# A hybrid decoder layer on one core, with and without six groups of constant products on TensorE

## The reference

```python
u = rmsnorm(x)
h = x + concat(gated_delta_net(u), rg_lru(u)) @ w_out       # 4 heads of 128; 4 blocks of 128
h = h + cross_attention(rmsnorm(h), rmsnorm(mem))           # 4 heads, 256 memory tokens
h = h + moe(rmsnorm(h))                                     # top 4 of 32 clamped-SwiGLU experts
out = rmsnorm(h)

def expert_block(x, e):                                     # blocks of 128 rows of one expert
    gt = minimum(x @ w_gate[e] + b_gate[e], 7.0)
    up = clip(x @ w_up[e] + b_up[e], -7.0, 7.0)
    return ((up + 1.0) * (gt * sigmoid(1.702 * gt))) @ w_down[e] + b_down[e]
```

## Time and profile before

| | us |
|---|---|
| median of 3 executions | 1771.23 |
| lowest, highest | 1770.09, 1771.25 |
| profiled execution, its own time | 1772.93 |
| span of the profiled execution | 1771.2 |
| TensorE busy | 1690.2 (95%) |
| VectorE busy | 1437.0 (81%) |
| ScalarE busy | 1274.6 (72%) |
| GpSimd busy | 527.8 (30%) |

### The profile page before, as it was taken

How to read it: one execution, slowest core, us unless ns; L and a number is a source line. 1 busy time by engine, 2 the same in 40 slices (tenths; PEclk the granted TensorE clock), 3 DMA queues, 4 the chain that set the end, 5 groups by cost and what they waited for, 6 DMA issues and landing times.

```text
span 1771.2 us, 24520 instructions
## 1 busy us (share of the span) xinstructions
PE 1690.2 (95%) x8065; PEld 1385.7 (78%) x8065; DVE 1437.0 (81%) x1531; ACT 1274.6 (72%) x1452; POOL 527.8 (30%) x624
## 2 busy tenths in 40 slices
PE   6999799899899989999999999999999999999997
PEld 3778598787768768888888888888888888888885
DVE  3558686663347969999999999999999999999997
ACT  4453454464435668888888888888888888888885
POOL 3453552200022822242222222232232323232232
PEclk9999999999998989999999999999999999999999
DMA  7312100042014879999999999999999999999993
GB/s 249 119 51 100 41 1 1 24 190 95 26 82 191 330 271 369 360 383 378 355 371 371 382 359 370 360 382 379 351 371 369 379 364 369 360 380 379 353 371 120
DMA packets 53880, 476.18 MB, mean 269 GB/s; under 512 B 10503, under 2 KB 11640, under 8 KB 29266
## 3 DMA queue, kind: packets, MB, share of 16 engines
q1 hardware_dynamic: 42528, 450.70, 62.8%
q0 software_dynamic: 11120, 24.91, 6.3%
q10 hardware_dynamic: 194, 0.06, 0.0%
HBM read 461.24 MB, written 23.08 MB: 273 GB/s over the span
## 4 chain that ended last, share of the span: by engine, by line
PE 61%; DVE 18%; issue 12%; ACT 6%; POOL 3%; DMA 1%; ACTq 0%; POOLq 0%; DVEq 0%
PE ps L1546 20%; PE ps L1506 17%; PE ps L1143 10%; PE ps L1304 4%; DVE wsp L1888 4%; DVE extra L2058 2%; DVE extra L2056 2%; DVE wsp_b L1888 2%; ACT extra L1048 2%; POOL extra L608 1%; PE ps L1533 1%; PE ps L1227 1%; DVE wf L1616 1%; PE ps L1239 1%; PE ps L1496 1%
## 5 line engine op out<-in xcount | busy, mean ns | idle before, releaser
L1888 DVE TENSOR_TENSOR wsp<-ring,wsp 128x1024 fp32r<-128x1024 f32 x512 | 601.1, 1219 | 26.6 <-ACT wsp L1003 26.1
L1003 ACT ACTIVATE wsp<-ring 128x1024 fp32r<-128x1024 f32 x388 | 387.0, 1051 | 80.2 <-PE ps L1488 53.0
L580 POOL TENSOR_TENSOR guard<-guard 1x1 f32<-1x1 f32 x219 | 133.8, 616 | 763.0 <-ACT extra L1071 327.9
L1506 PE MATMUL ps<-wsp,x_hi 128*128 128x512 f32 x1152 | 311.8, 392 | 0.6 <-DVE x_lo L2014 0.6
L1888 DVE TENSOR_TENSOR wsp_b<-ring,wsp_b 128x1024 fp32r<-128x1024 f32 x256 | 301.8, 1218 | 9.8 <-ACT wsp_b L1081 9.1
L1506 PEld LDWEIGHTS ps<-wsp,x_hi 128*128 128x128 f32 x1152 | 217.5, 189 | 50.1 <-issue 1.1
L1003 ACT ACTIVATE wsp_b<-ring 128x1024 fp32r<-128x1024 f32 x194 | 205.5, 1060 | 32.3 <-PE ps L1506 11.0
L1506 PE MATMUL ps<-wsp,x_lo 128*128 128x512 f32 x576 | 179.1, 392 | 0.0
L1616 DVE TENSOR_TENSOR wf<-ring,wf 128x1024 fp32r<-128x1024 f32 x64 | 81.3, 1273 | 111.8 <-ACT wf L713 111.8
L713 ACT ACTIVATE wf<-ring 128x1024 fp32r<-128x1024 f32 x80 | 84.2, 1055 | 117.4 <-PE ps L1143 62.2
L1143 PE MATMUL ps<-act_hi,wf 128*128 128x512 f32 x512 | 161.6, 397 | 2.6 <-DVE wf L1616 2.1
(11 more groups left out here) (380 smaller groups left out, 2993.9 us busy)
## 6 DMA issues: line engine op xcount, KB each, us to landing
ring<-in_w_gate_dram SPq DMA_DIRECT2D x32, 4096.0 KB, 15.3
ring<-in_w_up_dram SPq DMA_DIRECT2D x32, 4096.0 KB, 14.4
ring<-in_w_down_dram SPq DMA_DIRECT2D x32, 4096.0 KB
ring<-in_w_in_dram SPq DMA_DIRECT2D x6, 2048.0 KB, 12.0
ring<-in_w_ckv_dram SPq DMA_DIRECT2D x4, 2048.0 KB, 10.1
ring<-in_w_out_dram SPq DMA_DIRECT2D x2, 2048.0 KB, 10.6
ring<-in_w_cq_dram SPq DMA_DIRECT2D x2, 2048.0 KB, 11.1
ring<-in_w_co_dram SPq DMA_DIRECT2D x2, 2048.0 KB, 10.6
```

What stands on the lines that cost most here:

```text
L580: return pool.tensor_tensor(guard[:, i:i + 1], guard[:, 0:1], guard[:, 0:1], ALU.mult)
L1003: act.activation(split_w(c, 0), ring[:, m, k], ACT.Copy).then_inc(hi_ready, 1)
L1506: last = pe.matmul(ps[:, 2 * j + i], xp[:, k * P:(k + 1) * P], split_w(c, part)[:, i * 512:(i + 1) * 512], start=False, stop=(k == KT - 1 ...
L1888: dve.tensor_tensor(split_w(c, 1), ring[:, (GM + c // KT) % 3, c % KT], split_w(c, 0), ALU.subtract).then_inc(lo_ready, 1)
```

## The change

The helper and its six calls are taken out. The waits before and behind them stay, in their order, and so does every other instruction.

```diff
-            def fill_wait(n, bank):
-
-                for _ in range(n):
-                    pe.matmul(ps[:, bank, 0:2 * P], sel[:, 0], sel[:, :, :].rearrange("p j f -> p (j f)"), start=True, stop=True)
-
@@ heads of the delta net, h == 1
                     pe.wait_ge(kd_in, 1)
-                    fill_wait(30, 0)
@@ ahead of the solve's first transposes
             pe.wait_ge(kd_in, H)
-            fill_wait(34, 0)
@@ ahead of mixer_out(2)
             pe.wait_ge(orms_ready, H)
-            fill_wait(24, 0)
@@ i == 4
                     pe.wait_ge(onorm_ready, H)
-                    fill_wait(14, 4)
                     pe.wait_ge(al_ready, A_DN)
@@ cross attention
-            fill_wait(20, 6)
             prob_transposes(NT - 1)
@@ behind the router
-            fill_wait(12, 1)
             pe.wait_ge(oh_ready, 1)
```

## The result

Without the products the kernel takes 1773.28 us (median of 14; 1772.60 to 1775.39), with them 1770.19 us (median of 14; 1767.47 to 1772.71). The ratio is 1.0019, 95% interval 1.0011 to 1.0027: slower by 3.1 us between the medians, 1.9 to 4.8 us by the interval. In the profiled executions the spans are 1771.6 and 1771.2 us, only 0.4 apart. The profiled execution of the kernel before took 1772.93 us, 2.7 above the median of its fourteen and above the slowest of them; that of the changed kernel took 1773.40, 0.1 above its median. So this pair of profiles shows where time is lost, and not how much the change costs.

What follows compares the result with a forecast made beforehand. Bound: a full TensorE for two thirds, started by a serial front part of some 630 us. Terms 1.9 + 1.2 + 0.9, dropping the 0.1 us direct gain, made 4.0 us: 1771.23 to 1775.2 us, range 1771.0 to 1781.0.

Steps and rivals of the forecast that it cites:

- No direct gain: All six waits: the 18.4 us of products hide under other engines' work; removing them gives back at most 0.1 us.
- Group 1: 30 products ahead of the second head's key products: without them the clock falls and heads run at half rate, 1.9 us.
- this work is one third transposes, so I allow it one and a half heads: Heads from 198.1 us: how many run at half clock, averaging 0.8 us for one and 3.1 for two into 1.9.
- Group 5: 20 products at 477.37 us: eight transposes behind them 0.9 us slower, products of L1395 0.3 us more; together 1.2 us.
- Executions in which the fall doesn't happen today: Behind groups 4 and 5: where the clock holds today, the change costs 1.7 us more; at one in four each, 0.9.
- Groups 2, 3, 4: 34 products done at 212.1 us, 24 at 308.36, 14 at 317.52: slower work there stays covered by waits; cost 0.
- four stretches: TensorE at half clock (1.2 GHz) at 217.3 to 224.0, 323.1 to 326.4, 483.6 to 486.8 and 627.6 to 633.6 us.
- Group 6: 12 products at 561.72 us: L1458 starts cold, but L1474 ends just in time for VectorE's L2018; cost 0, upper bound 4.4.
- Whatever the front part loses arrives at the end one for one: Serial front part of some 630 us: its delays pass on whole, as the loop has 4 us in 1000 to give back.
- B: Rival, heads behind 198.1 us and L1395: low clock outlasts mixed work, 1778.7 us, or 1783.1 with a later bound; chance 0.22.
- C: Rival, 311.9 to 322.92 us: earlier fall shortens the idle, so 48 products run warm; faster, 1769.4 us; chance 0.06.
- A: Rival, not measurably slower: one cold head 0.8 us plus slow transposes at 481.30 us 0.9, 1772.9 us; chance 0.27.

## Why the prediction was right, and where it wasn't

Forecast 1775.2 us, 4.0 us more, in the range of 1771.0 to 1781.0; measured 1773.28, 3.1 us more (1.9 to 4.8). The mechanism is the forecast one; that the sum came within 1 us is in part luck, as the terms show.

- **No direct gain.** Right. The second head starts at 198.16 in both kernels, and the other resumptions follow their releasers as closely as before (the last transposes start 0.06 us behind VectorE's L1873 before, 0.05 behind its L1862 after).
- **Group 1, 1.9 us.** The mechanism is right to the detail (first bank in time, second bank 0.51 us late, third 0.16), the size is wrong. The clock was back at 203.5, so one head was slow, not one and a half: 0.87 us at VectorE, 0.80 us in the kernel without group 1. The step that failed is "this work is one third transposes, so I allow it one and a half heads". The row said that transposes in short bursts, with pauses, were followed by a fall, and I let them count for less than products; the kernel with 34 transposes shows that they keep the clock up. By itself the group measured +0.1 us (-1.2 to +2.1), so that its share of the 3.1 is not known.
- **Group 5, 1.2 us.** The transposes' 0.9 us came out (0.83). The stretch behind them lasted to 490.2, 5.8 us into L1385, not 4.25: L1385 took 1.30 us more than the 15.70 of the kernel before, and 3.0 more than the 14.00 where the clock held. So the group was under-sized in this pair (2.1 us), and by its median it carries over half of the change (+1.7 us by itself, 0.5 to 3.5).
- **Executions in which the fall doesn't happen today, 0.9 us.** Right in kind, and shown at 483: no fall in four of seven, where I had one in four. At 323 the clock fell in all seven kernels with group 4 as it was, so that half of the term was nothing.
- **Groups 2, 3, 4 at 0.** Right: ratio 0.9998. The new stretch at 313 lies under a wait, as reckoned.
- **Stretches left out.** The reading of four stretches missed the ones at 541.5 and 562.0 in the kernel before, at the router and at group 6. The router's is the one that made the pair of profiles differ by so little.
- **Group 6 at 0.** The table's product, L1463 in the changed kernel (L1474 before), ends at 581.0 in the changed kernel, and L2007 (L2018 before) starts at 582.00, no idle before it; so that wait was reckoned rightly. The positions were put at nothing without a reason, and they are 0.17 us longer in this pair, and 0.5 longer than where the clock is up. By itself the group measured +0.7 us with 0 at the edge of the interval; not settled.
- **"Whatever the front part loses arrives at the end one for one".** Wrong as stated. Work that is late meets the same return of the clock at 224.0, 326.4 and 633.6 with less of itself left to do slowly: 0.85 us became 0.56 by 323 and 0.43 by 481. From 1.05 at 582 to 0.4 at the end it shrank too, but 0.44 of that is the faster bias DMA. Too much at group 1 and this missing discount on one side, too little at group 5 on the other, nearly cancelled.
- **Rivals.** B (the low clock outlasts the heads) is out: the second slow head never came. C is out: its fall at 313 did happen and the 24 products ended later, but the idle before 323.48 was still 3.63 us and the clock fell again. A's price, 0.8 + 0.9, was the right one for the two first terms; it left out the longer stretch in L1385.

## What to carry to other kernels

TensorE work in a wait is not wasted when it is off the path: ask for each such group what runs in the first microseconds behind it, and whether that is the path. Here one of six places carried over half of the 3 us by the medians, three together were worth nothing, and covering the pauses that were left was worth 8 to 9. Before adding or removing such work, list the stretches at half clock with what TensorE does in them; half the products did as well as all of them, and a single pair of profiles misled by 2.7 us on the total.

## What the runs showed of the hardware

- In the pair of profiles the granted clock came back at 224.1, 326.5 and 633.7 us in the kernel before and within 0.2 us of that in the changed one, with the work 0.85 to 0.56 us apart: the return did not follow the work. Across executions it lies elsewhere (the return near 224 was at 222.7 to 227.5 us in those profiles of the experiments that have one).
- Executions of the kernel before spread over 7 us (1766.85 to 1774.09 us, all chips), and the granted clock of an execution goes with it. Of the 82 beside the experiments, the 13 at a mean clock of 0.990 have a median of 1768.2 us, the 29 at 0.988 one of 1770.6, the 10 at 0.987 one of 1771.8, the 4 at 0.986 one of 1773.5. Those of the changed kernel, whose profile has the clock down at each of the six, spread over 2.8 us at 0.979 to 0.982.
- Float32 transposes back to back hold the full clock (1.00 from 190 to 213 us with 34 of them in the wait, and a mean of 0.9886 over 11 executions against 0.9885). The Trainium skill, page "TensorE: Matmul & The Clock Gate", section "Part 4: PE-mode transpose", says they don't count; this trace disagrees.
- Products of 32 columns ran at full rate behind a filled pause, sixteen in 1.97 us instead of 2.77, in both profiles that fill it; with the pause of 2.2 us left as it is, in four of twelve.
- The DMA of one expert's bias took 2.95 to 4.65 us at the same place of the program in fourteen profiles, and TensorE waits for it.
- 15 products with 1.5 us of silence on either side held the clock in the one execution that was profiled, and 2 us of them replace 3.9.
